# Four-row gate products spread among the products of a feature chunk

## The reference, cut to what matters

```python
z = rms_norm(x, norm_mix_w) @ w_in + b_in        # q, k, v of both mixers, output gates, 8 gate columns
ig, fg = z[..., COL_MI:COL_MF], z[..., COL_MF:COL_GA]      # 4 heads each
lf = log_sigmoid(fg)
bcum = cumsum(lf)
dmat = bcum[..., :, None] - bcum[..., None, :] + ig[..., None, :]     # causal
m_t = maximum(max(dmat, axis=-1), m_inter)
p = exp(dmat - m_t[..., None]) * einsum('bhcld,bhcsd->bhcls', q, k)
h = (p @ v + ...) / maximum(abs(den), exp(-m_t))
```

## Time and profile before

| | |
|---|---|
| median of 3 runs | 1965.95 us (1965.41 to 1969.41) |
| profiled execution, its own time | 1970.17 us |
| its span, first to last instruction | 1968.3 us |
| mean granted TensorE clock | 0.995 |
| TensorE busy | 1933.9 us, 98% of the span |
| VectorE, ScalarE, GpSimd busy | 1377.6, 925.8, 238.1 us |
| chain that ended last | PE 87%, DVE 8%, ACT 2%, issue 2% |

### The profile page before, as it was taken

One profiled execution on the slowest core, in us unless ns is written; L12 is line 12 of the kernel. 1 busy time (PEld: TensorE's weight loads), 2 busy tenths in 40 slices (PEclk: granted clock), 3 DMA queues, 4 the chain that ended last, 5 costly groups with the idle time before them and its releaser, 6 DMA issues.

```text
span 1968.3 us, 29916 instructions
## 1 busy us (share of the span) xinstructions
PE 1933.9 (98%) x11936; PEld 1728.0 (88%) x11936; DVE 1377.6 (70%) x1577; ACT 925.8 (47%) x1020; POOL 238.1 (12%) x196
## 2 busy tenths in 40 slices
PE   7999999999999999999999999999999999999998
PEld 6999888889998888888799988888888799998887
DVE  7686766668677666666679677666666669676666
ACT  5554443346545445444554445444444554545443
POOL 0000000000001000000058250000000049250000
PEclk9999999999999999999999999999999999999999
DMA  7544555554356554555444455555555454454553
GB/s 265 199 152 150 192 186 189 186 189 170 129 200 216 188 186 161 201 192 192 145 167 154 174 187 195 190 190 173 185 188 192 154 178 151 171 193 163 190 192 107
DMA packets 50481, 353.35 MB, mean 180 GB/s; under 512 B 5920, under 2 KB 6048, under 8 KB 8656
## 3 DMA queue, kind: packets, MB, share of 16 engines
q1 hardware_dynamic: 47952, 341.93, 49.4%
q0 software_dynamic: 2432, 10.04, 1.6%
HBM read 349.85 MB, written 2.10 MB: 179 GB/s over the span
## 4 chain that ended last, share of the span: by engine, by line
PE 87%; DVE 8%; ACT 2%; issue 2%; DMA 0%; DVEq 0%; POOL 0%; SPq 0%; POOLq 0%; ACTq 0%
PE ps L225 18%; PE ps L189 18%; PE ps L190 17%; PE ps L191 17%; PE ps L226 9%; PE ps L229 3%; DVE w_lo L165 3%; PE ps L228 1%; ACT w_hi L158 1%; DVE conv_y L2000 1%; DVE a L1792 1%; ACT a L1562 1%; PE ps L1184 1%; DVE score L2048 0%; DVE top L2043 0%
## 5 line engine op out<-in xcount | busy, mean ns | idle before, releaser
L165 DVE TENSOR_TENSOR w_lo<-raw,w_hi 128x2048 fp32r<-128x2048 f32 x318 | 736.9, 2321 | 295.9 <-ACT w_hi L158 295.0
L158 ACT ACTIVATE w_hi<-raw 128x2048 fp32r<-128x2048 f32 x318 | 607.9, 1916 | 365.9 <-PE ps L191 222.2
L225 PE MATMUL ps<-a,w_hi 128*128 128x512 f32 x1568 | 563.0, 398 | 2.3 <-DVE GU L1875 1.3
L226 PE MATMUL ps<-a,w_lo 128*128 128x256 f32 x1568 | 439.9, 281 | 0.0
L225 PEld LDWEIGHTS ps<-a,w_hi 128*128 128x128 f32 x1568 | 295.0, 188 | 66.8 <-issue 3.1
L189 PE MATMUL ps<-mixH,w_hi 128*128 128x256 f32 x1168 | 335.8, 288 | 0.5 <-DVE w_lo L165 0.3
L190 PE MATMUL ps<-mixL,w_hi 128*128 128x256 f32 x1168 | 331.8, 284 | 0.0
L191 PE MATMUL ps<-mixH,w_lo 128*128 128x256 f32 x1168 | 331.8, 284 | 0.0
L189 PE MATMUL ps<-w_hi,mixH 128*128 128x512 f32 x832 | 324.4, 390 | 1.0 <-DVE mixL L397 0.9
L190 PE MATMUL ps<-w_lo,mixH 128*128 128x512 f32 x832 | 323.7, 389 | 0.0
L191 PE MATMUL ps<-w_hi,mixL 128*128 128x512 f32 x832 | 323.7, 389 | 0.0
(11 more groups left out here) (376 smaller groups left out, 2255.5 us busy)
## 6 DMA issues: line engine op xcount, KB each, us to landing
raw<-in_w_b SPq DMA_DIRECT2D x198, 1024.0 KB, 4.9
raw<-in_w_a SPq DMA_DIRECT2D x125, 1024.0 KB, 4.8
rows<-in_post_gains POOLq DMA_DIRECT2D x6, 512.0 KB, 4.1
rows<-in_rows_a POOLq DMA_DIRECT2D x2, 1028.0 KB, 6.8
raw<-in_w_a SPq DMA_DIRECT2D x2, 512.0 KB, 6.5
x<-in_x SPq DMA_DIRECT2D x2, 512.0 KB, 6.4
bias_line<-a_gates POOLq DMA_DIRECT2D x1, 1024.0 KB, 4.2
out<-x SPq DMA_DIRECT2D x4, 256.0 KB, 2.0
```

Of the source, the lines that this page charges most:

```text
L158: act.activation(k.w_hi[:, s, :], k.raw[:, s, :], ACT.Copy).then_inc(k.hi_ready, 1)
L165: dve.tensor_tensor(k.w_lo[:, s, :], k.raw[:, s, :], k.w_hi[:, s, :].bitcast(F32), ALU.subtract).then_inc(k.lo_ready, 1)
L225: pe.matmul(both, hi[:, kt, cols], k.a[:, :, kt, :], start=kt == 0, stop=False)
L226: pe.matmul(high, lo[:, kt, cols], k.a[:, 0, kt, :], start=False, stop=False)
```

## The change

`f_chunk` gets an argument `beside`, a function that it calls behind each `product` but the last, with the product's number from 0 to 14. The burst is no longer issued ahead of `feature(6, 15)`; it is handed to it as `gate_rows`. Behind products 0 to 3 stands one of the four-row products (two passes), behind products 4 to 7 one transpose each, behind products 8 to 14 nothing. The waits for `rows_ready` and `logit_ready` stand behind product 0, and `nm_done` is raised by the transpose behind product 7, half way through the chunk. The number of instructions on TensorE stays the same, and so do their operands and banks. No other engine's program is touched.

```diff
-def f_chunk(k, pe, c, banks, rows, act, pairs_ready=None, tiles=2):
+def f_chunk(k, pe, c, banks, rows, act, pairs_ready=None, tiles=2, beside=None):
...
                 end = product(pe, out, (hi[:, kt, cols], lo[:, kt, cols]), act(kt), i == 0, i == len(kts) - 1)
+                if beside is not None and (n, i) != (tiles - 1, len(kts) - 1):
+                    beside(n * len(kts) + i)
...
-                def feature(i, c):
+                def feature(i, c, beside=None):
...
-                    f_chunk(k, pe, c, [i % 2], [range(8)], nop)
+                    f_chunk(k, pe, c, [i % 2], [range(8)], nop, beside=beside)
...
-                pe.wait_ge(rows_ready.sem, rows_ready.at(l, 1))
-                pe.wait_ge(logit_ready.sem, logit_ready.at(l, 1))
-                for h in range(MH):
-                    pe.matmul(k.ps[:, 4 + h // 2, (h % 2) * SEQ:(h % 2 + 1) * SEQ], sel[:, h, :], g_rows[:, 2, :],
-                              start=True, stop=True)
-                for i, row in enumerate((1, 3)):
-                    for tt in range(TT):
-                        ins = pe.transpose(k.ps[:, 6, (2 * i + tt) * MH:(2 * i + tt + 1) * MH], g_rows[:, row, tt * P:(tt + 1) * P], k.ident[0:MH, 0:MH])
-                ins.then_inc(nm_done.sem, 1)
-                feature(6, 15)
+                def gate_rows(i):
+
+                    if i == 0:
+                        pe.wait_ge(rows_ready.sem, rows_ready.at(l, 1))
+                        pe.wait_ge(logit_ready.sem, logit_ready.at(l, 1))
+                    if i < MH:
+                        pe.matmul(k.ps[:, 4 + i // 2, (i % 2) * SEQ:(i % 2 + 1) * SEQ], sel[:, i, :], g_rows[:, 2, :],
+                                  start=True, stop=True)
+                    elif i < MH + 2 * TT:
+                        a, tt = (i - MH) // TT, (i - MH) % TT
+                        ins = pe.transpose(k.ps[:, 6, (2 * a + tt) * MH:(2 * a + tt + 1) * MH],
+                                           g_rows[:, 1 + 2 * a, tt * P:(tt + 1) * P], k.ident[0:MH, 0:MH])
+                        if (a, tt) == (1, TT - 1):
+                            ins.then_inc(nm_done.sem, 1)
+
+                feature(6, 15, gate_rows)
```

## The result

The changed kernel takes 1976.32 us (median of 6 runs, 1975.11 to 1977.15) against 1967.0 us of the kernel before in the same comparison (6 runs, 1963.89 to 1969.41): ratio 1.0044, 95% interval 1.0033 to 1.0055. It is slower by 9.3 us between the medians. The profiled execution is the slowest of the six (1977.15) and has a span of 1975.4 us, 7.1 over the profiled one of before.

The account below looks back on a forecast made before the run. TensorE, busy 98% of the span, was taken as the bound. From 1970.17: -3.0 + 5.4 + 2.6 + 0.2 = 1975.4; from the median 1965.95 without the gain, 1974.2, or 1971.2 with it; 1973.5 us taken, range 1969.0 to 1976.5.

Parts of the forecast that it names:

- Seams: TensorE, at changes between 128 and four rows: uncovered weight loads add 2.7 us a layer, 5.4 in all.
- The clock: TensorE during the spread items: granted clock falls again, once a layer, perhaps twice; 1.3 us each, 2.6 in all.
- What goes away: TensorE behind the old burst: the slow stretch at 1.2 GHz ends, 1.5 us a layer, 3.0 in all.
- the starting point: Time of the kernel before from which terms were summed: median of three runs, 1965.95 us, guessed free of slow stretches.
- The wait behind `nm_done`: VectorE waits 3.3 us for the later signal; TensorE 0.3 us a layer unless slow clock covers it; 0.2 taken in all.
- (a): Rival, TensorE: the clock stays up, uncovered loads at row changes are paid; 1969.0 to 1972.0 us, chance 0.20.
- (b): Rival, TensorE: single row changes are hidden, clock stays up; 1963.0 or 1966.0 us, chance 0.17 shared with (c).
- (c): Rival: row changes hidden but VectorE's chain bounds, costing 0.2 us at most; 1966 us, chance 0.17 shared with (b).
- (d): Rival: VectorE's next stage is late again at `wt_ready`, up to +1 us, inside the range; no separate chance given.

Follow-up runs that it names:

- experiment 1: Changed kernel with 64 rows instead of 4 in each inserted product, transposes made products with four columns: 1971.97 us, ratio 1.0023 to the kernel before.
- experiment 2: Changed kernel with 128 rows in each inserted product, transposes made products with four columns, so no row count changes: 1966.49 us, ratio 0.9994 to before.
- experiment 8: The changed kernel timed and traced again, nothing altered, beside the other follow-up kernels: 1977.91 us, ratio 1.0046 to before.
- Experiment 6: Kernel before, burst in place, the four products widened to 128 rows, the four transposes left at 4 rows: 1965.38 us, ratio 0.9990 to before.
- experiment 3: Kernel before, burst in place, 128 rows in the four products and in the transposes, which become two-pass products: 1965.46 us, ratio 0.9990 to before.
- experiment 7: Kernel before, burst in place, products and transposes all with 128 rows, transposes in one pass, VectorE's copy strided: 1965.08 us, ratio 0.9984 to before.
- experiment 4: Kernel before, four-row burst kept whole but issued behind product 7, half way through feature chunk 15: 1967.75 us, ratio 0.9999 to before.
- experiment 5: Kernel before, four-row burst split in two groups: four products behind product 0, four transposes behind product 7: 1969.33 us, ratio 1.0005 to before.

## Why the prediction was right, point by point

The direction and the two causes were right, and 1976.32 lies in the range, but only 0.2 us under its upper end and 2.8 over the number; the second measurement, 1977.91, lies above that end. Two terms were mis-sized, in opposite directions, and a choice beside them went wrong. That the number came so near owes something to luck, as the point on luck shows.

**Seams: right in kind, a little too large.** An item with a product was 1.18 us as forecast. An item with a transpose was 0.70 at full clock, not 0.79. Full-clock path from these: 0.36 + 4 x 1.18 + 4 x 0.70 + 7 x 0.36 + 0.12 = 10.5 us, against 8.2 before: 2.3 us a layer where the forecast had 2.7. The prediction put 0.11 for the transpose's own load and 0.12 to the load behind it; the load of 128 rows in fact starts 0.15 after the transpose (495.62 to 495.77). The upper bound of this term, 5.9, took the 0.34 paid before off only once; for two layers it is 5.6. The sentence of the Trainium skill ("TensorE: Matmul & The Clock Gate", on packing small matmuls) that a load overlaps with running matmuls only when the row group differs, read strictly, would have made the seams free; experiments 1 and 2 decide against that reading: with equal rows the load is ahead of its matmul and an item costs 0.79, with unequal ones 1.18.

**The clock: the right event, a good third of its size.** The forecast had one slow stretch anew in each layer, 1.3 us each, 2.6 in all, "perhaps twice". Measured: 14.75 - 10.5 = 4.2 us in layer 0 and 13.36 - 10.5 = 2.9 in layer 1, 7.1 in all. The price of one stretch was right: 4.2 for three and 2.9 for two is 1.4 us each. Their number was not: five in all instead of two. The same two lengths in experiment 8 show that this wasn't chance in one execution. Why the lower clock lasts longer here is not shown. What the traces show is that it fell while the items were still running (at 106.8 us, before the first transpose at 108.62), that the items left then took 1.13 instead of 0.70 us, so that there was four-row and uncovered-load time for longer, and that it came back 5.0 us after the last four-row item (112.02 to about 117.0, 497.74 to about 502.7), against 3.6 and 3.8 after the burst of before. A slow clock that prolongs its own cause would fit this, but no run varied it by itself.

Experiment 6 shows that the seams of a burst aren't what brings the clock down, and experiment 1 that eight pairs don't either; taking rows from 4 to 64 in the same places takes the slow stretches away. Experiment 1 also turned the transposes into products. In the changed kernel's layer 0 the fall came before any transpose, so they aren't needed for it; whether they have a part in its length is open.

**What goes away: rightly 1.5 us a stretch, wrongly left out of the median.** The forecast took 3.0 us off for the two stretches of the profiled execution and then guessed from three runs that the median had none of them. The many runs of before bear out the size: their spans lie at 1962.6 to 1963.2 us where the mean granted clock is 0.998, and at about 1964.5, 1966.2 and 1967.8 where it is 0.997, 0.996 and 0.995, steps of 1.6 us. They don't bear out the guess. The median of 28 and 27 runs is 1967.9 to 1968.1, 2 us over that of the three runs, one step under the profiled execution and not two. And the kernels that lose the slow stretches behind the burst gain what the traces of before and of these kernels say for both layers: 2.4, 3.1 and 3.3 us by the path in experiments 3, 6 and 7, and 2.4, 2.7 and 3.0 by the median. So the usual execution of before did pay for most of the 3.0, though the intervals of these gains are wide (0.2 to 3.7 us in experiment 6).

**Where luck helped.** From 1973.5 to 1976.3 are 2.8 us. The clock alone was 4.5 too low, and the starting point 1.1 (1967.0, not 1965.95). Against these stood the seams, 0.8 too high, and the gain that the number left out almost whole, some 2.3. With the measured terms the sum is 1967.0 - 3.0 + 4.6 + 7.1 = 1975.7, so the account closes to 0.6 us; the forecast came near it by errors that partly cancelled.

**The wait behind `nm_done`: rightly nothing.** VectorE waited 5.2 us (3.3 forecast; the slow clock again) and TensorE none: L1141 starts 0.12 behind the last product. The forecast had said that a slow stretch covers it. Where the clock stays up and `nm_done` comes late the wait is there, 0.29 to 0.38 us in experiments 1, 2, 4 and 5, against 0.3 worked out.

**The rivals.** (a), clock up and seams paid, is what experiment 1 is, but not what the change did. That its 1971.97 meets the 1972.0 worked out is chance: it is 4.1 over its own kernel before, where the rival had 6.0 over 1965.95. (b), seams hidden when single, is refuted by every item. (c) is close to experiment 2, which removes the seams: 8.84 us a layer, no loss and no clear gain. (d), VectorE late at `wt_ready`, didn't show; no later wait of TensorE on that chain is in the trace of after.
